# A modulation sum behind a score level, head scaling before centring, and part of the first output mix ahead of the last retention block

## What is computed

```python
mod = (jax.nn.silu(cond) @ w_ada + b_ada)[:, None, :]          # 6 x 1024 per condition
sh1, sc1, g1, sh2, sc2, g2 = jnp.split(mod, 6, axis=-1)
h = rmsnorm(x, norm1_w) * (1 + sc1) + sh1
proj = h @ w_in                                                # q, k, v, gates of both groups
...
o = o_f + flip_seq(o_b)                                        # retention, 4 heads
mu = jnp.mean(o, axis=-1, keepdims=True)
var = jnp.mean(jnp.square(o - mu), axis=-1, keepdims=True)
o_ret = merge_heads((o - mu) * lax.rsqrt(var + EPS)) * ret_norm_w * silu(rg)
...
o_gla = merge_heads(u * lax.rsqrt(mean(u * u) + EPS)) * gla_norm_w * silu(gr)
mix = jnp.concatenate([o_ret, o_gla], axis=-1) @ w_out
x = x + g1 * mix
```

## Time and profile before

| | |
|---|---|
| Median of 3 runs | 832.17 us (832.07 to 835.92) |
| Profiled execution, its own time | 833.67 us |
| Its span (first to last instruction) | 831.9 us |
| PE busy | 725.4 us (87%), 4297 instructions |
| DVE busy | 393.4 us (47%), 782 instructions |
| POOL busy | 206.9 us (25%) |
| ACT busy | 155.7 us (19%) |
| Loaded and stored | 186.02 MB, mean 224 GB/s |
| Mean granted TensorE clock | 0.94 of full speed |

### The profile page before, as it was taken

One profiled execution on the slowest core, in us unless ns is written; L12 is line 12 of the kernel. 1 busy time (PEld: TensorE's weight loads), 2 busy tenths in 40 slices (PEclk: granted clock), 3 DMA queues, 4 the chain that ended last, 5 costly groups with the idle time before them and its releaser, 6 DMA issues.

```text
span 831.9 us, 10844 instructions
## 1 busy us (share of the span) xinstructions
PE 725.4 (87%) x4297; PEld 467.4 (56%) x4297; DVE 393.4 (47%) x782; ACT 155.7 (19%) x257; POOL 206.9 (25%) x239
## 2 busy tenths in 40 slices
PE   3899996999999999999899999889999777788730
PEld 1655553558888565677788885455554433344310
DVE  0462399587576675656734335712233112111227
ACT  2320421011322215313101111111111001001002
POOL 1500044233333101112300000124444323323213
PEclk8989898999999999999999999999999999989975
DMA  9945304322233434335249317949999999999955
GB/s 353 369 146 155 102 1 137 117 82 94 79 102 102 131 123 137 103 118 144 71 180 404 155 51 299 369 143 368 374 380 384 397 387 389 394 390 385 386 199 240
DMA packets 74307, 186.02 MB, mean 224 GB/s; under 512 B 10012, under 2 KB 47044, under 8 KB 65296
## 3 DMA queue, kind: packets, MB, share of 16 engines
q1 hardware_dynamic: 62688, 159.94, 52.3%
q0 software_dynamic: 6144, 12.83, 4.7%
q10 hardware_dynamic: 5424, 12.55, 4.0%
HBM read 174.48 MB, written 17.10 MB: 230 GB/s over the span
## 4 chain that ended last, share of the span: by engine, by line
PE 61%; DMA 12%; DVE 11%; SPq 8%; issue 3%; ACT 2%; POOL 2%; DVEq 0%; POOLq 0%; ACTq 0%
PE bank L1633 18%; DMA weights_x_h<-in_expert_w_up 10%; PE bank L1850 7%; PE bank L1796 7%; PE bank L1623 4%; PE bank L1866 4%; SPq L525 3%; DVE qkv_gates_tables L1113 3%; SPq L524 3%; SPq L528 2%; DMA weights_x_h<-in_w_ada 2%; PE bank L1661 2%; PE bank L1752 2%; PE bank L1743 2%; PE bank L1695 2%
## 5 line engine op out<-in xcount | busy, mean ns | idle before, releaser
L1633 PE MATMUL bank<-weights_x_h 128*128 128x128 f32 (+3 forms) x672 | 190.7, 445 | 1.4 <-DVE weights_x_h L1079 1.4
L1633 PEld LDWEIGHTS bank<-weights_x_h 128*128 128x128 f32 (+1 forms) x672 | 103.5, 191 | 89.6 <-issue 88.2
L1850 PE MATMUL bank<-qkv_gates_tables,attention 128*64 128x256 f32 x480 | 59.4, 403 | 16.5 <-DMA qkv_gates_tables<-in_expert_w_up 15.6
L1448 DVE TENSOR_TENSOR attention<-attention,bank 128x128 f32<-128x128 f32 x32 | 9.2, 288 | 135.8 <-ACT attention L992 135.8
L1623 PE MATMUL bank<-weights_x_h 128*128 128x256 f32 x320 | 70.3, 380 | 0.0
L1623 PEld LDWEIGHTS bank<-weights_x_h 128*128 128x128 f32 x320 | 60.4, 190 | 9.3 <-DVE attention L1097 0.8
L1850 PE MATMUL bank<-weights_x_h,attention 128*64 128x256 f32 x416 | 52.2, 408 | 13.6 <-DMA weights_x_h<-in_expert_w_up 13.6
L1796 PE MATMUL bank<-weights_x_h 128*128 128x256 f32 x256 | 57.8, 388 | 0.0
L1850 PEld LDWEIGHTS bank<-qkv_gates_tables,attention 128*64 128x64 f32 x480 | 35.6, 146 | 35.9 <-DMA qkv_gates_tables<-in_expert_w_up 17.2
L635 POOL TENSOR_TENSOR small<-small 128x1 f32<-128x1 f32 (+1 forms) x20 | 15.7, 783 | 153.9 <-DVE small L1033 153.9
L1796 PEld LDWEIGHTS bank<-weights_x_h 128*128 128x128 f32 x256 | 49.6, 195 | 7.0
(11 more groups left out here) (286 smaller groups left out, 997.9 us busy)
## 6 DMA issues: line engine op xcount, KB each, us to landing
weights_x_h<-in_w_ada SPq DMA_DIRECT2D x24, 1024.0 KB, 7.7
qkv_gates_tables<-in_expert_w_gate SPq DMA_DIRECT2D x15, 1024.0 KB, 19.0
qkv_gates_tables<-in_expert_w_up SPq DMA_DIRECT2D x15, 1024.0 KB, 27.2
qkv_gates_tables<-in_expert_w_down SPq DMA_DIRECT2D x15, 1024.0 KB, 26.7
weights_x_h<-in_w_in SPq DMA_DIRECT2D x14, 1024.0 KB, 7.6
weights_x_h<-in_expert_w_gate SPq DMA_DIRECT2D x13, 1024.0 KB, 20.9
weights_x_h<-in_expert_w_up SPq DMA_DIRECT2D x13, 1024.0 KB, 26.4
weights_x_h<-in_expert_w_down SPq DMA_DIRECT2D x13, 1024.0 KB, 26.6
```

The lines of the kernel that those rows point to most:

```text
L1633: ins = mm(ps[0:m, 0:hi - lo], wt[:, k, c * m:(c + 1) * m], hT[:, k, lo:hi], start=(k == 0), stop=(k == KC - 1))
L1850: ins = mm(bank[2 + n][j * SLOTS:(j + 1) * SLOTS, 0:2 * P], xte[n][:, k, :], exgu[b][:, :, k, j * P:(j + 1) * P], start=(k == 0), stop=(k ...
```

## The change

Three edits, all of order. No instruction is added or taken away.

1. VectorE's `combine(4)`, which stood after item 3's product, stands after item 4's, just before `combine(5)`. `sums_after` is unchanged, so TensorE still adds both after item 5.
2. In the `o` job of a retention block VectorE scales the block before it (`scaled`) first and centres the block (`centre`) then; before it was the other way round. The adding up of the squares stays last.
3. The four banks of the first mix are begun after the transpose of retention block 1 and before retention block 3, and chunks 4 and 5 of each quarter are added there; chunks 6, 7, 0 and 1 follow after block 3 as before, where the drains of transposes 0 and 1 are now awaited.

```diff
+def combined_after(i):
+
+    return {3: [], 4: rest_after(3) + rest_after(4)}.get(i, rest_after(i))
...
-        if job == ("o", "r", HEADS - 1):
+        if job == ("T", "r", 1):
             jobs += [("mix", 0, n) for n in range(4)]
...
-            dve_order += [("acc", r) for r in rest_after(i)]
+            dve_order += [("acc", r) for r in combined_after(i)]
...
-                dve_order += ([("cen", block)] if block[0] == "r" else []) + ([("on", BLOCKS_OUT[n - 1])] if n else []) + [("ms", block)]
+                dve_order += ([("on", BLOCKS_OUT[n - 1])] if n else []) + ([("cen", block)] if block[0] == "r" else []) + [("ms", block)]
...
-                for r in rest_after(i):
+                for r in combined_after(i):
                     combine(r)
...
                     n = BLOCKS_OUT.index(b)
+                    if n:
+                        scaled(BLOCKS_OUT[n - 1])
                     if b[0] == "r":
                         centre(b)
-                    if n:
-                        scaled(BLOCKS_OUT[n - 1])
                     squares(b)
...
-                if job == ("o", "r", HEADS - 1):
+                if job == ("T", "r", 1):
                     first = [starts(("mix", 0, n)) for n in range(4)]
                     for h in range(HEADS):
                         is_drained(te, ("T", "g", h))
+                    for n in range(4):
+                        load_ready(te, LOADS.index(("out", n)))
+                        first_mix(n, [4, 5])
+                elif job == ("o", "r", HEADS - 1):
                     is_drained(te, ("T", "r", 0))
                     is_drained(te, ("T", "r", 1))
                     for n in range(4):
-                        load_ready(te, LOADS.index(("out", n)))
-                        first_mix(n, [4, 5, 6, 7, 0, 1])
+                        first_mix(n, [6, 7, 0, 1])
```

## The result

The changed kernel takes 821.16 us (median of 4 runs, 820.18 to 821.43); the kernel before took 832.78 beside it (4 runs, 832.07 to 835.92). The ratio is 0.984, 95% interval 0.982 to 0.986: 1.6% faster, and 0.8 us above the 820.4 forecast. The profiled execution took 821.39 with a span of 819.6.

What follows compares the result with a forecast made beforehand. TensorE was taken to bound the kernel up to the stream of expert weights. Edit 1's 8.3 plus 3.4 for edits 2 and 3 make 11.7 us off the 832.17 median: 820.4, own bounds 818.4 to 823.6.

Steps and rivals of the forecast that it cites:

- Edit 1: Level 0 to item 6: TensorE's 8.22 us stop goes and item 6 begins at 161.2, saving 8.3 us (6.2 to 10.2).
- the rotations behind sum 5: Four VectorE instructions after sum 5 free the banks for level 1 and item 6: 2.9 to 4.8 us, 3.9 taken.
- the prediction's own queue: On SP, item 6's weights stand behind the load waiting for sum 4; they land at 160.9 (160.4 to 161.4).
- The contention: VectorE's sums 4 and 5, each beside one GpSimd product, lose between nothing and 2 us together; 1 taken.
- The price that the prediction worked out from the rule: Sums 4 and 5: GpSimd's two products cost VectorE their full length, 2.9 us, leaving edit 1 a saving of 6.4.
- Edits 2 and 3: Around retention blocks 1 to 3: the 3.35 us gap before the transpose is filled, saving 3.4 us (2.4 to 3.6).
- The filler: Transpose (0.5 us) and drawn-forward mix instructions (3.5) fill 409.9 to 413.8, so block 3 begins where it did.
- The context block's scaling: On VectorE it waits 0.5 us for GpSimd's root, hidden because its transpose runs only behind four score matmuls.
- A: Sums 4 and 5 keep 11.3 us each: edit 1 loses 1.8, the whole gains 1.6, 830.6 us; chance 0.15.
- C: Before block 3 the filler isn't hidden: edits 2 and 3 give nothing and 823.9 us is left; chance 0.05.
- B: TensorE's clock falls again between 156 and 161: price 1.3 plus 1 us, 9.4 saved, 822.8 us; chance 0.12.
- D: Slower: item 6's weights, queued behind sum 4, come so late that the kernel takes 836.4 us or more; chance 0.05.

Runs made afterwards that it cites:

- edits23_alone: The changed kernel with edit 1 undone, so sum 4 stays ahead of level 0; 830.72 us, ratio 0.995 to the kernel before.
- edit3_alone: The kernel before with only chunks 4 and 5 of the first mix drawn forward, centring still ahead of scaling; 833.30 us, ratio 1.000.
- rotations_first: The changed kernel with sum 4 moved between the two rotations and level 0's copies; 820.31 us, ratio 0.984 to the kernel before.
- swap_sums: The changed kernel with sum 5 ahead of sum 4 behind level 0; 830.45 us, ratio 0.996 to the kernel before.
- three_chunks: The changed kernel with three first-mix chunks (4, 5 and 6) ahead of retention block 3 in place of two; 821.12 us, ratio 0.984 to the kernel before.
- edit1_alone: The changed kernel with edits 2 and 3 undone, only sum 4 moved behind level 0; 826.63 us, ratio 0.992 to the kernel before.
- split_sum: The changed kernel with the first 6 of sum 4's 16 instructions ahead of the product lqk(1); 817.96 us, ratio 0.982 to the kernel before.

## Why the prediction was right

**Edit 1, 8.3 forecast, 8.85 measured** (7.9 where the clock fell). Counted from level 0's start, which came 1.74 sooner, the steps were forecast at 134.7, 139.3, 148.9, 155.5 and 159.5 (item 5, lqk(1), ends of sums 4 and 5, item 6) and stood at 134.69, 139.34, 149.25, 155.32 and 158.90. The term that was off most is the rotations behind sum 5, 3.9 forecast, 3.5 measured (155.24 to 158.75): their SBUF additions took 1.05 and 0.98, not the 1.65 of the earlier trace rows. Sum 5 ended 0.2 us sooner than forecast; the two make the 0.6. The range's best end for this edit, 10.2, contradicts the prediction's own queue: weights that land at 160.4 at the earliest leave 9.1 at most.

**The contention, 1 us forecast for both sums, 1.0 measured**, all of it on sum 4, where half on each was assumed; that the total came out is in part luck. GpSimd's two products, one beside each sum:

```profile
142.54 1.28 POOL L689 TENSOR_TENSOR qkv_gates_tables<-qkv_gates_tables 128x512 f32<-128x512 f32 x1 [5.60 <-ACT qkv_gates_tables L885]
...
152.05 4.41 POOL L689 TENSOR_TENSOR qkv_gates_tables<-qkv_gates_tables 128x512 f32<-128x512 f32 x1 [8.23 <-ACT qkv_gates_tables L885]
```

Beside sum 4 the product took 1.28 and the sum lost 1.0; beside sum 5 the sum lost nothing and the product took 4.41. One of the two pays, not always VectorE. The Trainium skill (page "SBUF — State Buffer", section "Who interferes with whom") says that issue order decides which engine is blocked; the two rows agree with that: the first product began at 142.54, just ahead of sum 4's fourteen instructions (142.61), the second at 152.05, in the midst of sum 5's. Its rule blocks an engine for one instruction of the other, and a sum's instruction is 0.40 us (5.62/14), where the product grew by 3.1 (it took 4.15 to 4.66 in five other profiles with the two sums in one piece): there the measurement decides. The price that the prediction worked out from the rule, 2.9 us on VectorE, was not paid.

**Edits 2 and 3, 3.4 forecast and 3.6 at most, 3.88 measured.** The filler fits as forecast: from the transposes to block 3 it is 3.89 us (398.88 to 402.77), and from block 2's end to block 3 it was as long before (409.9 to 413.79). The tail from the mix behind block 3 to the expert load fell from 12.43 to 8.99, 3.44. The other 0.44 lies between item 6 and that mix and was not in the sum; edits23_alone has it without edit 1. Of it 0.30 lies in two steps from one head block to the next, which were 9.38 us before (385.66, 395.04, 404.42) and are 9.23 (375.05, 384.28, 393.51). It is edit 2's: edit3_alone keeps 9.38. The context block's scaling waited as forecast, 0.47 us at 372.54, and the transpose that wants it ran without a gap at 374.61.

**Sum and end.** What was won by 158.90 was still there at the expert load. From there on the kernel's own scatter, about 4 us between the extremes, is as large as edits 2 and 3. Both terms were larger than forecast, 12.73 us in the profiles for 11.7, and yet the median came out 0.8 above the forecast. Of that 0.6 is the base: the forecast was counted from 832.17, and the median of before was 832.78 with one run more. From median to median the gain is 11.62, so that the 11.7 agrees to a tenth is luck within the scatter.

**The rivals.** A didn't come: sum 4 took 7.2 us, not 11.3. Its reason stands all the same, as rotations_first paid 9.1 beside the subtractions. C is excluded by edits23_alone, where edits 2 and 3 gained their whole 3.87.

B came in part and not always: the granted clock from 158 to 160 was 1.00 in one profile of the changed kernel and 0.50 in the other, 27.83 against 26.88. With the 0.46 that item 6 then loses behind the mark (258.67 against 258.21) its price is 1.4 us, not 2.3. It was argued as one case or the other; it differs from execution to execution of the same kernel. The row from 94 to 96 that the prediction took as its precedent is a poor one: TensorE was busy without a pause from 87.64 on, with 16 gate matmuls of 32 rows and 512 columns in 6.05 us, and the clock fell within them (0.64 from 90 to 92), so it shows a fall after steady work, not after short work. The Trainium skill (page "TensorE: Matmul & The Clock Gate", Part 1) says that how many matmuls run at the lower clock at a kernel's start differs between runs of one kernel; these two profiles show the like in the middle of one.

D's mechanism was shown by swap_sums; the margin against it, 0.3 us forecast, was 0.5, and that was luck. Sum 4 ended 0.4 later than forecast, and 10.3 us from there, as in the earlier trace rows, item 6's weights would have landed at 159.55 and cost 0.65; the load took 8.5 us in place of 9.7. In four other profiles with this order of the sums it took 8.0 to 9.4, and with 9.4, in three_chunks, TensorE did wait 0.60 for it. Item 5's weights, which the prediction set aside since nothing moves them, were as close: they landed at 134.7 (issued at 125.19, 9.5 us), and TensorE, now there earlier, waited 0.17 for them.

## What to carry to other kernels

When a long block of work is moved past short steps that free another engine's buffers, price the short steps' start, not the block's length: the whole gain of edit 1 was that four instructions of 0.7 us came first. Two waits in a row on one engine need both edits, since removing the first alone moves the time to the second and filling the second alone fills nothing. And before two equal steps change places, look at what is queued in program order behind the loads that wait for each.

## What the runs showed of the hardware that was not expected

A gap of 3.35 us left TensorE's clock at full level in the kernel before (block 3's first group behind it took 1.06 us) and in edit3_alone (1.05), but not in edit1_alone (1.91, granted 0.58 from 406 to 412), where the slower stretch behind it cost 2.8 us. So a gap of this length can cost itself or nearly twice itself. What decides between the two was not settled; each is seen in one or two profiles.

GpSimd's product of 128x512, 1.28 us in one place, took 4.41 beside sum 5 in the changed kernel and 2.14 in split_sum, where less of it lies beside the sum (sum 5 ends 1.0 us after its start there, 3.3 in the changed kernel). The kernel before had it already: 2.45 for the product that began at 155.11, 1.3 us before sum 5's end. In all three the product ended 1.1 us after the sum's last instruction, however early it had begun: beside a run of VectorE instructions with no pause, GpSimd was held over several of them, nearly until the run ended.
